# Delta rule of a hybrid backbone: key norm and beta folded into per-token columns, key products once per token tile, the mask as one rounded product

## The reference

```python
q = l2norm(to_heads(q, 4)) * 128 ** -0.5          # l2norm(x) = x * rsqrt(sum(x*x) + 1e-6)
k = l2norm(to_heads(k, 4))
beta = sigmoid(raw[0]);  g = -exp(a_log) * softplus(raw[1] + dt_bias)

gc = cumsum(g)                                    # inside a chunk
decay = exp(where(incl, gc[:, None] - gc[None, :], -inf))
kb = k * beta[:, None]
a_low = where(strict, (kb @ k.T) * decay, 0)
rhs = concatenate([v * beta[:, None], kb * exp(gc)[:, None]])
u, w = split(solve(a_low + eye, rhs))             # unit lower triangular
attn = (q @ k.T) * decay
q_dec = q * exp(gc)[:, None]
k_dec = k * exp(g_last - gc)[:, None]
# over chunks:
v_new = u - w @ state
o = q_dec @ state + attn @ v_new
state = state * exp(g_last) + k_dec.T @ v_new

o = rmsnorm(o, w)                                 # per head, then times silu(z)
```

## Time and profile before

| | us |
|---|---|
| median of 3 runs | 2286.82 |
| lowest and highest | 2283.01, 2290.33 |
| profiled execution, first to last instruction | 2282.3 |
| TensorE busy in it | 2104.3 (92%) |
| VectorE busy | 1449.3 (64%) |
| ScalarE busy | 1122.0 (49%) |
| GpSimd busy | 209.2 (9%) |
| mean granted TensorE clock | 0.967 of 2.4 GHz |

### The profile page before, as it was taken

How to read it: one execution, slowest core, us unless ns; L and a number is a source line. 1 busy time by engine, 2 the same in 40 slices (tenths; PEclk the granted TensorE clock), 3 DMA queues, 4 the chain that set the end, 5 groups by cost and what they waited for, 6 DMA issues and landing times. The chain is left out here.

```text
span 2282.3 us, 27862 instructions
## 1 busy us (share of the span) xinstructions
PE 2104.3 (92%) x11070; PEld 1718.0 (75%) x11070; DVE 1449.3 (64%) x1437; ACT 1122.0 (49%) x1252; POOL 209.2 (9%) x219
## 2 busy tenths in 40 slices
PE   3999998998699999989987899999999999999994
PEld 2667567998588888878765688888788878878783
DVE  3651375446743223356856688888888888888884
ACT  3221252221442222244335577777777777777773
POOL 0100102324100000012521000000000000000001
PEclk8999999999799999999997899999999999999997
DMA  8667311000337442323005699999999999999994
GB/s 314 226 261 274 149 52 40 2 1 1 111 103 239 133 117 74 111 93 94 1 1 185 235 370 380 372 369 376 354 381 368 373 364 368 372 369 365 372 372 150
DMA packets 246377, 507.17 MB, mean 222 GB/s; under 512 B 11998, under 2 KB 80791, under 8 KB 239847
## 3 DMA queue, kind: packets, MB, share of 16 engines
q1 hardware_dynamic: 242791, 491.17, 59.9%
q0 software_dynamic: 3456, 14.16, 1.6%
HBM read 485.34 MB, written 19.96 MB: 221 GB/s over the span
## 5 line engine op out<-in xcount | busy, mean ns | idle before, releaser
L134 DVE TENSOR_TENSOR arena_r<-arena,arena_r 128x2048 fp32r<-128x2048 f32 (+2 forms) x456 | 928.1, 2049 | 349.7 <-ACT arena_r L130 349.2
L130 ACT ACTIVATE arena_r<-arena 128x2048 fp32r<-128x2048 f32 (+2 forms) x456 | 779.5, 1723 | 326.3 <-DMA arena<-in_moe_w 241.3
L2430 PE MATMUL bank<-arena_r,gate_rows_r 128*128 128x512 f32 x896 | 351.8, 393 | 0.0
L139 PE MATMUL bank<-hT_r,arena_r 128*128 128x512 f32 (+1 forms) x688 | 262.7, 382 | 15.7 <-DVE arena_r L134 13.1
L2428 PE MATMUL bank<-arena_r,arena_r 128*128 128x512 f32 x672 | 267.5, 398 | 0.0
L2429 PE MATMUL bank<-arena_r,arena_r 128*128 128x512 f32 x672 | 261.6, 389 | 0.0
L140 PE MATMUL bank<-catT_r,arena_r 128*128 128x512 f32 (+1 forms) x688 | 260.1, 378 | 0.0
L141 PE MATMUL bank<-hT_r,arena_r 128*128 128x512 f32 (+1 forms) x688 | 260.0, 378 | 0.0
L2430 PEld LDWEIGHTS bank<-arena_r,gate_rows_r 128*128 128x128 f32 x896 | 169.5, 189 | 36.6
L2459 PE MATMUL bank<-arena_r,hT_r 128*128 128x512 f32 x448 | 177.9, 397 | 15.6 <-DVE catT_r L2552 13.9
L2461 PE MATMUL bank<-arena_r,catT_r 128*128 128x512 f32 x448 | 174.7, 390 | 0.0
(11 more groups left out here) (393 smaller groups left out, 3040.5 us busy)
## 6 DMA issues: line engine op xcount, KB each, us to landing
arena<-in_moe_w SPq DMA_DIRECT2D x336, 1024.0 KB, 6.1
gate_rows<-in_ada_w SPq DMA_DIRECT2D x40, 1024.0 KB, 7.6
arena<-in_ffn_w SPq DMA_DIRECT2D x44, 512.0 KB, 5.2
arena<-in_ev_w_in SPq DMA_DIRECT2D x14, 1024.0 KB, 5.5
arena<-in_ffn_w SPq DMA_DIRECT2D x11, 1024.0 KB, 4.8
arena<-in_od_w_in SPq DMA_DIRECT2D x9, 1024.0 KB, 5.2
arena<-in_ada_w SPq DMA_DIRECT2D x8, 1024.0 KB, 17.4
expert_rows_in<-ada_bias_rows SPq DMA_DIRECT2D x8, 1024.0 KB, 7.2
```

The source lines that it names most:

```text
L130: return act.activation(rounded(hi), v, ACT.Copy)
L134: return dve.tensor_tensor(rounded(v), v, rounded(hi).bitcast(F32), ALU.subtract)
L139: pe.matmul(acc, xh_, wh_, start=start, stop=False)
L2430: mm = pe.matmul(out_bank, lo, wh[:, k, :], start=False, stop=(kk == KD - 1))
```

## The change

The norm block is gone, and `FX` keeps queries and keys as the convolution left them. With r the inverse norm of a key, the reciprocal of its squared norm (`LNM`) is r squared, and `M = BETA * LNM` is beta times r squared. The triangular system is rescaled by beta times r on both sides, which leaves in it the plain key products times the decay times `M` of the source token. So the exponential's bias becomes `ln(M) - GC` in place of `-GC`, values are multiplied by the key's norm 1/r (`NK`) in place of beta, the keys for W by `EGC` alone, and the exponent of the state's keys gets `ln(M)` too (`EKM`). The queries' factor comes in at the gate norm: squared and over 128 (`RQ2`) into the sum of squares, and once (`q_cols(RN)`) into the result. Since beta sits in the bias, the products keys times keys and keys times queries are the same for both directions, and the groups are done tile by tile with the directions inside. The mask and the identity are rounded once in the first block to `exact_const` (both hold values that rounding leaves as they are), so that the mask product is one rounded product, here and in the SSD.

The core of the diff:

```diff
+        exact = ctx.enter_context(nc.sbuf_tensor("exact_const", [P, 3 * P], F32R))
+        ident_r, neg_r = exact[:, 0:P], (exact[:, P:2 * P], exact[:, 2 * P:3 * P])
...
             @block.scalar
             def _(act):
+                act.wait_ge(s_const, 16)
+                act.activation(ident_r, ident, ACT.Copy)
+                for d in range(2):
+                    act.activation(neg_r[d], cst(f"neg{d}"), ACT.Copy)
                 act.wait_ge(s_trc, 1)
...
                 pool.wait_ge(s_sse, 1)
-                link(pool.tensor_tensor(RL, RL, mhalf[:, 0:32], ALU.pow))
-                queries = RL.rearrange("p (i c) -> p i c", c=8)[:, :, 0:4]
-                pool.tensor_scalar(queries, queries, float(P) ** -0.5, None, ALU.mult).then_inc(s_rl, 1)
+                link(pool.tensor_tensor(RN, RL, mhalf[:, 0:32], ALU.pow))
+                link(pool.tensor_scalar(q_cols(RN), q_cols(RN), float(P) ** -0.5, None, ALU.mult))
+                pool.tensor_tensor(by_tile(NK), k_cols(RL), k_cols(RN), ALU.mult)
+                link(pool.tensor_tensor(by_tile(RQ2), q_cols(RN), q_cols(RN), ALU.mult))
+                pool.tensor_scalar(RQ2, RQ2, 1.0 / P, None, ALU.mult).then_inc(s_rl, 1)
...
-        s_bc, s_nrm = sem("dn_rnorm_spread"), sem("dn_normed")
-        with nc.Block() as block:
...
-            @block.tensor
-            def _(pe):
-                for c in range(8):
-                    if c >= 4:
-                        pe.wait_ge(s_nrm, c - 3)
-                    for i in range(T):
-                        mm = pe.matmul(bank[1 + c % 4][:, i * P:i * P + P], RL[:, 8 * i + c:8 * i + c + 1].to_broadcast([P, P]), ident,
-                                       start=True, stop=True)
-                    mm.then_inc(s_bc, 1)
-
-            @block.vector
-            def _(dve):
-                for c in range(8):
-                    dve.wait_ge(s_bc, c + 1)
-                    dve.tensor_tensor(FX[:, c, :], FX[:, c, :], bank[1 + c % 4][:, :], ALU.mult).then_inc(s_nrm, 1)
```

The columns block of the delta rule is written out anew. TensorE's list is that of `columns_and_turns`; SyncE's six loads move into it; the lists of VectorE and ScalarE are:

```diff
+            @block.vector
+            def _(dve):
+                link = linker(dve, "dve")
+                both = lambda v: v.rearrange("p (i d h) -> p i d h", i=T, d=2)
+                link(dve.reciprocal(by_tile(LNM[:, 0:16]), k_cols(RL)))
+                dve.wait_ge(s_gt, 1)
+                dve.tensor_copy(GS, bank[0][:, 32:64]).then_inc(s_gcp, 1)
+                link(dve.tensor_copy(BETA, bank[0][:, 0:32]))
+                link(dve.tensor_scalar(BETA, BETA, 1e-25, None, ALU.max))
+                dve.tensor_tensor(both(M), both(BETA), LNM[:, 0:16].rearrange("p (i d h) -> p i d h", i=T, d=1).to_broadcast([P, T, 2, 4]), ALU.mult).then_inc(s_m, 1)
+                copy(dve, 1, s_kvv, 0, 4)
+                dve.wait_ge(s_cs, 1)
+                link(dve.tensor_copy(GC, bank[1][:, 0:32]))
+                link(dve.tensor_copy(GL, bank[1][:, 32:64]))
+                dve.wait_ge(s_ln, 1)
+                link(dve.tensor_tensor(BIAS, M, GC, ALU.subtract))
+                dve.tensor_tensor(EKM, GL, BIAS, ALU.add).then_inc(s_bi, 1)
+                copy(dve, 1, s_kvv, 4, 8)
+
+            @block.scalar
+            def _(act):
+                act.wait_ge(s_m, 1)
+                act.activation(M, M, ACT.Ln).then_inc(s_ln, 1)
+                copy(act, 0, s_kva, 0, 4)
+                act.wait_ge(s_bi, 1)
+                for dst, src in ((EGC, GC), (EGL, GL), (EKM, EKM)):
+                    act.activation(dst, src, ACT.Exp).then_inc(s_ex, 1)
+                copy(act, 0, s_kva, 4, 8)
```

The mask block (VectorE's and ScalarE's loops follow the same order of `n`, with `BIAS` in place of `NGC`), the block of U and W, the gate norm and the SSD:

```diff
             @block.tensor
             def _(pe):
-                for d in range(2):
-                    for h in range(4):
-                        j = 4 * d + h
-                        if j >= 2:
-                            pe.wait_ge(s_kb, j - 1)
-                        for i in range(T):
-                            mm = pe.matmul(bank[6 + j % 2][:, i * P:i * P + P], col(BETA, i, d, h).to_broadcast([P, P]), ident, start=True, stop=True)
-                        mm.then_inc(s_bs, 1)
...
+                for n in range(8):
+                    i, d = divmod(n, 2)
+                    tk = slice(i * P, i * P + P)
+                    if n >= 2:
+                        pe.wait_ge(s_dt, n - 1)
+                    pe.matmul(quad(n % 2), ident_r, neg_r[d].rearrange("p (a c) -> p a c", a=1).to_broadcast([P, 4, P]), start=True, stop=False, skip_group_check=True)
                     for h in range(4):
-                        mm = pe.matmul(quad(g % 2)[:, h, :], col(GS, i, d, h).to_broadcast([P, P]), cum[d], start=False, stop=(h == 3), skip_group_check=True)
+                        mm = pe.matmul(quad(n % 2)[:, h, :], col(GS, i, d, h).to_broadcast([P, P]), cum[d], start=False, stop=(h == 3), skip_group_check=True)
                     mm.then_inc(s_pd, 1)
...
+                    if d == 0:
+                        if i >= 2:
+                            pe.wait_ge(s_am, 2 * i - 2)
+                        for h in range(4):
+                            mm = pe.matmul(quad(2 + i % 2)[:, h, :], FX[:, 4 + h, tk], FX[:, 4 + h, tk], start=True, stop=True)
+                        mm.then_inc(s_pa, 1)
+                        if i >= 2:
+                            pe.wait_ge(s_qm, 2 * i - 2)
+                        for h in range(4):
+                            mm = pe.matmul(quad(4 + i % 2)[:, h, :], FX[:, 4 + h, tk], FX[:, h, tk], start=True, stop=True)
+                        mm.then_inc(s_pq, 1)
...
                 for g in range(9):
-                    if g < 8:
-                        if g >= 2:
-                            dve.wait_ge(s_pu, g - 1)
-                        dve.tensor_tensor(heads(BV[:, g % 2, :], 4), heads(VT[:, g % T, :], 4), spread(gcol(BETA, g), 4, P), ALU.mult).then_inc(s_bv, 1)
+                    if g < T:
+                        dve.tensor_tensor(heads(VT[:, g, :], 4), heads(VT[:, g, :], 4), spread(NK[:, 4 * g:4 * g + 4], 4, P), ALU.mult).then_inc(s_bv, 1)
...
-                dve.tensor_reduce(orr, osq, AX.X, ALU.add).then_inc(s_oss, 1)
+                link(dve.tensor_reduce(orr, osq, AX.X, ALU.add))
+                dve.tensor_tensor(orr, orr, RQ2, ALU.mult).then_inc(s_oss, 1)
                 dve.wait_ge(s_or, 1)
+                link(dve.tensor_tensor(by_tile(orr), by_tile(orr), q_cols(RN), ALU.mult))
...
-                            pe.matmul(quad(q % 2), ident, neg[d].rearrange("p (a c) -> p a c", a=1).to_broadcast([P, 4, P]), start=True, stop=False, skip_group_check=True)
+                            pe.matmul(quad(q % 2), ident_r, neg_r[d].rearrange("p (a c) -> p a c", a=1).to_broadcast([P, 4, P]), start=True, stop=False, skip_group_check=True)
```

121 lines of the change are left out of this document (68 added, 53 removed).

## The result

The changed kernel takes 2244.33 us (median of four runs, 2242.37 to 2245.01), against 2285.51 us for the kernel before on the same chip. The ratio is 0.9819, with a 95% interval of 0.9805 to 0.9834. The forecast was 2254 us with a range from 2245 to 2265, so the direction is right, and the gain is larger than said: 41.2 us between the medians and 39.1 between the profiled executions, against 32.6 in the sum. The time lies 0.7 us under the range. A second set of runs of the same two kernels gave 2246.39 us and 0.9828 [0.9809, 0.9847].

The account below looks back on a forecast made before the run. One core runs fenced blocks, each ended by its latest engine, TensorE in the delta rule. Savings of 8.4 + 0 + 18.0 + 1.75 - 0.4 + 4.9 = 32.6 us took the 2282.3 us span to 2249.7; plus 4.5, 2254 us, range 2245 to 2265.

Parts of the forecast that it names:

- Part 1: Norm block ahead of the gates' transposes: removing it saves 8.43 us.
- part 2: Columns block: an extra table load stays hidden and small changes cancel, 0 us; bounds 0.2 gained, 1.3 lost.
- Part 3: Delta rule's mask block: shared key products and a rounded mask product shorten it to 18.84 us, saving 18.0 us.
- B: Rival: rounding the mask product brings nothing, in mask block and SSD scan; gain 22.9 us, 2264 us; chance 0.09.
- Part 4: Block of U and W: with fewer VectorE products beside them, GpSimd's last four groups speed up, saving 1.75 us.
- Part 5: Gate norm: two added linked VectorE operations lose 0.4 us; roundings and extra GpSimd columns elsewhere stay covered, 0.
- Part 6: SSD scan: the rounded mask product shortens each step by 1.24 us, saving 4.9 us over 4 steps.
- C: Rival: clock falls to 1.2 GHz for the mask block's first third or so, 6 us less gain, 2260; chance 0.11.
- S: Rival: clock stays down past the masks into the inversion, making the kernel slower, 2350 us; chance 0.01 with the like.
- Nothing in the new mask block leaves TensorE idle: Mask block: the reason given against a lower clock lasting into the inversion; no size of its own.
- what one block saves moves all that follows forward: Whole kernel: blocks end at barriers, so block savings pass fully to the total; 32.6 us in the sum.
- the 4.5 us between span and median: Whole kernel: the median lay 4.5 us above the profiled span, and this distance was added to 2249.7 us.

Follow-up runs that it names:

- after_keys_twice: The changed kernel with key-key and key-query products made again for every group in both directions; 2256.41 us, ratio 0.9895.
- after_delay_long: The changed kernel with 59 small linked VectorE operations as a delay ahead of layer 1's second half; 2274.96 us, ratio 0.9964.
- after_keys_on_vector: The changed kernel with the last four groups' state-key products (`EKM`) moved from GpSimd to VectorE; 2244.64 us, ratio 0.9823.
- round_only: The kernel before with only mask and identity rounded, for the mask product in the mask block and the SSD scan; 2270.5 us, ratio 0.9940.

## Why the prediction was right and where it failed

**Part 1, norm block, and part 2, columns: right.** 8.4 us and about 0. The second table load ended 0.04 us before its activation, as the 0.03 of the earlier trace rows; the columns block took 340.61 - 334.66 = 5.95 us where 6 was said. The drain that the Trainium skill's page "ScalarE: Activation LUTs", section "What ACT_TABLE_LOAD costs", puts on top of a load is not there behind either of them: the logarithm starts 0.25 us after its load ended, right behind VectorE's product, and the exponentials 0.04 us after theirs.

**Part 3, mask block: right.** 18.89 us against 18.84. The tile is 4.04 to the hundredth; the mask product holds TensorE for 0.31 us rather than 0.24, but inside the pace of the tile only 0.24 shows. The two experiments that undo its halves cost about what they should, and B is excluded.

**Part 4, U and W: right mechanism, 0.75 us short.** Late groups fell from 2.44 to 1.99 us. At like clock the part is worth 1.8 us. What the term lacked was the start of the block, which now falls into 6.8 us at 1.2 GHz.

**Part 5, gate norm: -0.5 for -0.4. Part 6, SSD: 5.0 for 4.9.** A step of 6.67 us.

**The clock, rivals C and S: wrong place.** It held in the mask block, where C had it fall, and fell in the inversion, for 6.8 us at its start and 3.4 us at 376.9. "Nothing in the new mask block leaves TensorE idle" overlooked the end of the block, where the new order lets it stand still for 4.12 us instead of 2.35. In the eleven traces with 4.12 the clock falls at the start of the inversion each time, in the nine with 2.35 it falls in three. `after_keys_twice` is one of the nine, the only version of the changed kernel with 2.35, and has no stretch at the lower clock there. The stretch at the start costs nothing: `after_delay_long` and `after_keys_on_vector` have it for 6.8 us too, and their inversions take 137.4 us. In the second TensorE is busy 3.40 of 3.40 us, and half of that, 1.7, is the loss. The row from which I argued, 386 to 400 of the earlier trace rows, is the same work of the kernel before at 1.00, behind the shorter idle time. Why the second stretch comes in some versions and not in others is open. In U and W the clock cost 0.75; in the scan the changed kernel lacks a stretch of 3.4 us that the one of before has at 547.5, which gives back 1.6. The three nearly cancel, to -0.8 us. That they do is luck; no term foresaw them.

**The failed step: "what one block saves moves all that follows forward",** at the top, and with it the sum, which has no term for what comes after the SSD scan. The last sentence of the prediction names the case (a later stage, equal in its instructions, takes a different time), but gave it no size and no chance. It was 6.9 us. The change takes 208 matmuls and as many weight loads out of TensorE's list (the page counts 11070 and 10862 of each); that moves the place of the expert stage's code in the list, and two stops there, where its loop jumps back, shrink (3.55 us together in the first trace of before, 2.59 in that of the changed kernel, 4.00 and 1.81 in the second pair). `round_only`, with 32 instructions less and nothing else of the change, had this gain already (962.0 us). 32.6 + 6.9 - 0.8 = 38.7 of the 39.1 us.

**The range.** The forecast counted on the 4.5 us between span and median. They were not there: in all runs of this case the time lies 2.0 us above the execution's own span or less, and the 4.5 was the distance between the profiled execution and the median of three. That was the smaller error, 2 to 3 us on the side on which the time fell. The low end of 2245 allowed for it (2254 - 4.5 = 2249.5), which left 4.5 us for all else that could come better than said. The expert stage alone took 6.9.

**What stays open.** What decides how early before the jump the transfer of instructions begins, and so the rule by which the stops grow and shrink; how some 1 to 2 us of difference in the stops becomes 7 us of the stage, of which two windows of DMA share show 2.4; and why one stage with short stops took 966.2 us. That TensorE waits for the instructions themselves is what the fixed 2.8 to 2.9 us say in 40 stops; no run changed the transfer alone.

## What to carry to other kernels

In a kernel of fenced blocks, the difference of start times of the same instruction before and after, with the tail of the block taken over unchanged, prices a removed or thinned block to a tenth of a microsecond. A stage that is the same in its instructions is not thereby the same in time: after any edit that changes the length of an engine's list, look in the long stages behind it for idle time that names no releaser, at the jumps of its loops above all and together with the instruction queue, and keep some 0.3% of the time in the range for it. When the order in a block changes, look at how long its last engine leaves the others idle, too. Before work is moved off the engine that closes a block, read the busy time per step of the next one, since that is all that can be gained.

## What the runs showed of the hardware

- A rounded fp32 product of 128x512 among full fp32 ones costs 0.24 to 0.31 us of TensorE, the fp32 one 0.86.
- TensorE stops 0.6 to 2.1 us at two fixed places of the expert stage, without a wait. In 19 of the 20 traces, stops that sum to 3.2 us or more go with stages of 965 to 970 us, and sums of up to 3.0 with 960 to 963. Adding 96 unused instructions far ahead turned one into the other, in both directions.
- A stop of 2 us costs the stage about 3 us, since the transfers behind it dry up (DMA share 0.70 over 10 us).
- The same blocks, shifted by some 27 us, got the lower clock in other stretches: the inversion took 137.4 or 139.0 us, the scan 32.6 or 34.2, the block of U and W 19.7 or 20.5. A stretch of 3.4 us at 1.2 GHz on solid TensorE work costs half its length; beside other engines' work, nothing.
